# A decoder block with a PEER channel mixer on one Trainium2 core: groups of eight experts by column quarters, activations weighed and split in PSUM

## What is computed

```
q = a @ w_q                                   # a = rms_norm(h), 1024 tokens
s1, s2 = q0 @ k1.T, q1 @ k2.T                 # 8 heads, 128 keys each
top 16 of 128 x 128 sums per head -> idx, gate (softmax over the 16)
act = gelu(einsum('td,ted->te', xb, u[idx]))  # 128 experts of 16384 per token
out = einsum('te,ted->td', gate * act, v[idx])
```

## Time and profile before

| | us |
|---|---|
| median of 3 runs | 3580.4 |
| lowest, highest | 3580.07, 3585.87 |
| span of the profiled execution | 3575.0 |
| time of the median run less that span | 5.4 |
| mean granted TensorE clock, share of full | 0.983 |

### The profile page before, as it was taken

The page is one execution under the profiler, slowest core; times in us unless marked ns, Lnnn a source line. Parts: engine busy times, 40 slices in busy tenths (PEclk is TensorE's granted clock), DMA queues, the critical chain, the costliest instruction groups (busy, mean ns, idle before and its releaser), DMA issues.

```text
span 3575.0 us, 58964 instructions
## 1 busy us (share of the span) xinstructions
PE 3398.0 (95%) x22379; PEld 3333.7 (93%) x22379; DVE 2760.2 (77%) x4360; ACT 1201.3 (34%) x1885; POOL 2199.5 (62%) x1426
## 2 busy tenths in 40 slices
PE   7899989989999989999999999999999999999997
PEld 6899979988999979999999999999999999999975
DVE  5515467667887666999989899753898989998877
ACT  3310131232221232465665656542222222222242
POOL 5578865323678655666666666665666666666544
PEclk9999989999999999999999999999999999999998
DMA  4233432111688768889888988997888899988812
GB/s 152 79 117 123 136 108 79 56 49 65 215 311 313 279 217 290 281 307 326 310 324 303 335 304 323 322 354 258 314 309 312 310 312 314 315 311 311 282 60 94
DMA packets 326530, 856.15 MB, mean 239 GB/s; under 512 B 27856, under 2 KB 125648, under 8 KB 323024
## 3 DMA queue, kind: packets, MB, share of 16 engines
q0 software_dynamic: 110592, 402.70, 31.3%
q1 hardware_dynamic: 74592, 260.24, 21.5%
q10 hardware_dynamic: 141168, 190.87, 15.4%
HBM read 758.82 MB, written 94.90 MB: 239 GB/s over the span
## 4 chain that ended last, share of the span: by engine, by line
PE 71%; DVE 14%; issue 4%; DMA 3%; POOL 3%; ACT 3%; ACTq 1%; SPq 0%; DVEq 0%; POOLq 0%
PE main L720 52%; PE main L965 12%; PE scr L918 4%; DMA raw<-stream 3%; DVE scr L1729 2%; POOL v_lo L675 2%; POOL rows L626 1%; DVE rows L1722 1%; ACTq L1350 1%; DVE h L2104 1%; PE scr L818 1%; PE scr L735 1%; ACT v_hi L1360 1%; DVE res L2210 1%; DVE h_lo L2109 1%
## 5 line engine op out<-in xcount | busy, mean ns | idle before, releaser
L592 POOL TENSOR_TENSOR w_lo<-raw,w_hi 128x1024 fp32r<-128x1024 f32 x206 | 529.0, 2568 | 403.6 <-ACT w_hi L1064 397.7
L720 PE MATMUL main<-mix_hi,w_hi 128*128 128x320 f32 (+1 forms) x2816 | 684.7, 317 | 29.6 <-DVE mix_lo L1552 9.9
L720 PE MATMUL main<-mix_lo,w_hi 128*128 128x320 f32 (+1 forms) x2816 | 672.7, 313 | 0.0
L720 PE MATMUL main<-mix_hi,w_lo 128*128 128x320 f32 (+1 forms) x2816 | 672.6, 313 | 0.0
L626 POOL DMA_INDIRECT rows<-v_rows,s_idx x384 | 388.9, 1013 | 365.1 <-DVE scr L1729 290.9
L1729 DVE SCALAR_TENSOR_TENSOR scr<-rows,s_dot,scr 128x1024 f32<-128x1024 f32 x381 | 487.5, 1279 | 49.5 <-DMA rows<-v_rows,s_idx 31.5
L965 PE MATMUL main<-h_hi,v_hi 128*128 128x320 f32 x2048 | 473.2, 312 | 39.3 <-DVE res L2115 36.3
L720 PEld LDWEIGHTS main<-mix_hi,w_hi 128*128 128x128 f32 x2816 | 476.3, 189 | 34.0 <-issue 19.6
L720 PE MATMUL main<-a_hi,w_hi 128*128 128x320 f32 (+1 forms) x1728 | 466.7, 324 | 24.8 <-DVE a_lo L1552 8.8
L626 POOL DMA_INDIRECT rows<-u_rows,s_idx x384 | 399.0, 1039 | 137.0 <-issue 69.4
L720 PEld LDWEIGHTS main<-mix_lo,w_hi 128*128 128x128 f32 x2816 | 480.0, 189 | 0.0
(11 more groups left out here) (273 smaller groups left out, 5283.4 us busy)
## 6 DMA issues: line engine op xcount, KB each, us to landing
raw<-stream SPq DMA_DIRECT2D x478, 512.0 KB
act_d<-actb ACTq DMA_DIRECT2D x128, 320.0 KB
gate_d<-gbuf ACTq DMA_DIRECT2D x20, 2048.0 KB, 9.4
h<-act_d ACTq DMA_DIRECT2D x128, 320.0 KB
gate_in<-gate_d ACTq DMA_DIRECT2D x31, 1280.0 KB
rows<-u_rows,s_idx POOLq DMA_INDIRECT x384
rows<-v_rows,s_idx POOLq DMA_INDIRECT x384
score_d<-stage ACTq DMA_DIRECT2D x16, 320.0 KB
```

What stands on the lines that cost most here:

```text
L592: pool.tensor_tensor(w_lo[:, s, :], raw[:, s, :], w_hi[:, s, :].bitcast(F32), ALU.subtract) \
L720: last = pe.matmul(main[s][:, dst:dst + n], wt[:, s, c * P:(c + 1) * P], rows[:, c, src:src + n], start=(c == 0 and wt is w_hi and rows is ...
```

## The change

EG is 8: 16 groups, each of 8 column blocks ("steps", 128 in all) of 48 matmuls. V's tiles are laid out anew on the host: tile n of a group holds four experts by a quarter (256 columns) of the output, so a step pair needs two tiles, and only four tiles are held in v_hi and v_lo. h_hi, h_lo and h32 hold eight experts. Each expert's activations are copied by ACT into a PSUM place (`h_stage`, scr1), weighed there by DVE, cast from there by ACT, and the low half is the difference between it and h_hi. Gates are loaded for four experts at a time. All three sparse sums use scr0 and out0, and are turned into a place of `main` that counts as an item of its own between steps. Sparse rows before the V stage are 512, in it 256, with rings of 4 and 6 buffers. The first group's weighing moves into ACT's and DVE's loops at U tiles 119 to 126.

```diff
-EG = 4
+EG = 8
+HG = EG // 2
 NGRP = NE // EG
+V_STEPS = NGRP * DC
+PRE = 2
...
-LAST_ROWS = 2 * S1 + NE - 8
-SHIFT_ROWS = 2 * S1 + NE - 24
+LAST_ROWS = 2 * S1 + NE - 3
+SHIFT_ROWS = 2 * S1 + NE - 16
+FIRST_H = NE - EG - 1
+WEIGH_AT = ((), (0,), (1,), (2, 3), (4,), (5,), (6, 7), ())
+ROW_STEPS = V_STEPS - 5
 
 
...
-    return sum(RATES[:min(tile, LAST_ROWS)]) // 10
+    return min(sum(RATES[:min(tile, LAST_ROWS)]) // 10, UDOTS + P)
...
+def b_rows(step):
+
+    return A_DOTS + max(0, min(B_DOTS, B_DOTS * (step + 1) // ROW_STEPS))
...
+def target(step):
+
+    return UDOTS + P * (ENDS.index(step) + 1) if step in ENDS else b_rows(step)
...
+TURNS = [DC * ((ENDS[t] + 2 + DC) // DC) for t in range(NS - 1)] + [V_STEPS - 3]
...
-RING_B = (3, 4, 5, 7, 8, 9, 10, 11, 12)
+RING_END = (4, 5, 6, 7)
+RING_B = (4, 5, 8, 9, 10, 11)
...
-            v_hi.append(lay(f"v_hi{u}", [P, EG, D], F32R))
-            v_lo.append(lay(f"v_lo{u}", [P, EG, D], F32R))
+            at = set1 if u == 0 else set2
...
-            h32.append(nc.alloc_sbuf_tensor_at(f"h32_{u}", [P, EG, TDN], F32,
-                                               offset=(set1 if u == 0 else set2) + 42 * 1024))
-        gate_first = nc.alloc_sbuf_tensor_at("gate_first", [P, NBLK, EG, TB], F32, offset=tmp0)
-        v_raw = nc.alloc_sbuf_tensor_at("v_raw", [P, EG, D], F32, offset=set1 + 4 * K4)
...
             def fetch(n):
 
...
-                    while at_row[0] < to:
-                        gather()
+                to = min(target(n - 2) + 2, DOTS)
...
             pool.wait_ge(tile_done, 2 * B_PAIR)
-            pool.wait_ge(h32_ready, EG)
             for n in range(NE):
-                if n >= EG:
+                if n == PRE:
+                    pool.wait_ge(dot_done, A_DOTS)
+                if n >= PRE:
                     pool.wait_ge(v_hi_made, n + 1)
-                    pool.tensor_tensor(v_lo[n // EG % 2][:, n % EG, :], raw[:, n % 2, :],
-                                       v_hi[n // EG % 2][:, n % EG, :].bitcast(F32), ALU.subtract).then_inc(v_split, 1)
+                    pool.tensor_tensor(v_tile(v_lo, n), raw[:, n % 2, :], v_tile(v_hi, n).bitcast(F32),
+                                       ALU.subtract).then_inc(v_split, 1)
...
+            def turn_back(t):
...
+            def group(b, u, turns, last_turn=None):
                 for dt in range(DC):
-                    ahead_of(dt)
-                    slot = main[dt % 2]
-                    pe.wait_ge(b_drained, DC * b + dt + 1)
+                    if dt == last_turn:
+                        turn_back(turns)
+                        turns += 1
+                    quarter, of_two = divmod(dt, 2)
+                    slot = main[(dt + turns) % 2]
+                    pe.wait_ge(b_drained, DC * b + dt + turns + 1)
                     for k in range(EG):
+                        part, at = divmod(k, HG)
+                        n = 2 * quarter + part
+                        if of_two == 0 and at == 0:
+                            pe.wait_ge(v_split, EG * b + n + 1)
                         if dt == 0:
-                            pe.wait_ge(v_split, EG * b + k + 1)
                             pe.wait_ge(h_ready, EG * b + k + 1)
+                        col = at * 2 * P + of_two * P
                         for vt, ht in ((v_hi, h_hi), (v_hi, h_lo), (v_lo, h_hi)):
                             for half in range(2):
                                 last = pe.matmul(slot[:, half * HALF:half * HALF + HD],
-                                                 vt[u][:, k, dt * P:(dt + 1) * P],
+                                                 v_tile(vt, n)[:, col:col + P],
                                                  ht[u][:, k, half * HD:(half + 1) * HD],
                                                  start=(k == 0 and vt is v_hi and ht is h_hi),
                                                  stop=(k == EG - 1 and vt is v_lo))
                     last.then_inc(b_filled, 1)
...
             def v_cast(n):
-                b, k = divmod(n, EG)
-                act.wait_ge(raw_in[n % 2], 16 * (B_PAIR + (n - EG) // 2) + 16)
-                act.copy(v_hi[b % 2][:, k, :], raw[:, n % 2, :]).then_inc(v_hi_made, 1)
+                if n >= 4:
+                    act.wait_ge(b_filled, filled(2 * (n // 2 - 1)))
+                act.wait_ge(raw_in[n % 2], 16 * (B_PAIR + (n - PRE) // 2) + 16)
+                act.copy(v_tile(v_hi, n), raw[:, n % 2, :]).then_inc(v_hi_made, 1)
+
+            def h_stage(b, k):
+                act.wait_ge(act_in[k], 16 * b + 16)
+                if b or k:
+                    act.wait_ge(h_ready, EG * b + k)
+                act.copy(h_ps[:, 0:TDN], h32[b % 2][:, k, :]).then_inc(h_staged, 1)
 
             def h_cast(b, k):
                 act.wait_ge(h32_ready, EG * b + k + 1)
-                act.copy(h_hi[b % 2][:, k, :], h32[b % 2][:, k, :]).then_inc(hhi_ready, 1)
+                act.copy(h_hi[b % 2][:, k, :], h_ps[:, 0:TDN]).then_inc(hhi_ready, 1)
+                if k % HG == HG - 1 and b + 1 < NGRP:
+                    load_gates(b + 1, k // HG)
...
                 gelu(e)
+                if 0 <= e - FIRST_H < EG:
+                    h_stage(0, e - FIRST_H)
                 if e + 2 < NE:
                     after(A_PAIR + e // 2, e % 2)
+                if 0 <= e - FIRST_H < EG:
+                    h_cast(0, e - FIRST_H)
...
-            load_gates(1, gate_in)
-            act.wait_ge(dot_done, A_DOTS)
-            for k in range(EG):
-                load_act(1, k)
             act.wait_ge(gates_drained, 32 * ND + 2)
...
+            def sums_out(t):
+                act.wait_ge(dot_done, UDOTS + P * (t + 1))
...
+                act.copy(out0[:, :], acc[:, :]).then_inc(s_out, 1)
...
+            for b in range(NGRP):
+                for dt in range(DC):
+                    step = DC * b + dt
+                    if dt == 0 and b + 1 < NGRP:
+                        if b:
+                            act.wait_ge(b_filled, filled(step))
+                        for k in range(EG):
+                            load_act(b + 1, k)
+                    if step - 1 in ENDS:
+                        sums_out(ENDS.index(step - 1))
+                    ks = WEIGH_AT[dt] if b + 1 < NGRP else ()
+                    for k in ks[:1]:
+                        h_stage(b + 1, k)
+                    if dt % 2 == 0:
+                        for n in range(step + 2, min(step + 4, NE)):
+                            v_cast(n)
+                    for k in ks[:1]:
+                        h_cast(b + 1, k)
+                    for k in ks[1:]:
+                        h_stage(b + 1, k)
+                        h_cast(b + 1, k)
...
-                        acc = scr[ACC[t]]
+                        acc = scr[0]
...
             def weigh(b, k):
-                u = b % 2
-                gates = gate_in if b else gate_first
-                if k == 0:
-                    dve.wait_ge(gate_ins, 16 * (b + GATE_PARTS))
...
-                dve.tensor_tensor(h3, h3, gates[:, :, k, :], ALU.mult).then_inc(h32_ready, 1)
+                half = k // HG
+                if k % HG == 0:
+                    dve.wait_ge(gate_ins[half], 16 * (b + GATE_PARTS))
+                dve.wait_ge(h_staged, EG * b + k + 1)
+                h3 = h_ps[:, 0:TDN].rearrange("p (b t) -> p b t", t=TB)
+                dve.tensor_tensor(h3, h3, gate_in[half][:, :, k % HG, :], ALU.mult).then_inc(h32_ready, 1)
 
             def lo_of_group(b, k):
                 u = b % 2
                 dve.wait_ge(hhi_ready, EG * b + k + 1)
-                dve.tensor_tensor(h_lo[u][:, k, :], h32[u][:, k, :], h_hi[u][:, k, :].bitcast(F32), ALU.subtract) \
+                dve.tensor_tensor(h_lo[u][:, k, :], h_ps[:, 0:TDN], h_hi[u][:, k, :].bitcast(F32), ALU.subtract) \
...
-            def drain(b, dt):
...
+            def drain(step):
+                r = res[:, step % DC, TS:T].rearrange("p (a t) -> p a t", a=2)
+                dve.wait_ge(b_filled, 8 + item(step) + 1)
+                dve.tensor_tensor(r, main[item(step) % 2][:, :].rearrange("p (a t) -> p a t", a=2)[:, :, 0:HD], r,
+                                  ALU.add).then_inc(b_drained, 1)
 
...
             for k in range(EG):
+                rows_of(FIRST_H + k - 1)
                 weigh(0, k)
-            for k in range(EG):
+                dot_until(min(at_dot[0] + 1, A_DOTS))
                 lo_of_group(0, k)
...
+            dot(A_DOTS - at_dot[0])
+            weigh_sparse(2)
+
+            for step in range(V_STEPS - DC):
+                b, dt = divmod(step, DC)
+                if step in TURNS:
+                    add_sparse(TURNS.index(step))
+                drain(step)
+                for k in WEIGH_AT[dt]:
+                    weigh(b + 1, k)
+                    dot_until(min(at_dot[0] + 1, target(step)))
+                    lo_of_group(b + 1, k)
+                dot_until(target(step))
...
```

(29 more changed lines are left out.)

216 lines of the change are left out of this document (80 added, 136 removed).

## The result

The changed kernel takes 3611.9 us (median of 4 runs, 3604.47 to 3614.21); beside it, on the same chip, the kernel before takes 3580.35 us. The ratio is 1.0085, with a 95% interval of 1.0068 to 1.0102. The change makes the kernel slower by 0.9%, where 0.7% faster was forecast; the time lies outside the range.

The account below looks back on a forecast made before the run. TensorE, busy 95% of the 3575.0 us span, was taken as the bound, stopped by DVE's late drains. V stage -31.5, end of U +6, behind -1 gave 3548.5, plus 5.4 made 3554 us; range 3530 to 3583.

Parts of the forecast that it names:

- DVE relieved: V stage: halved drains and PSUM operands leave DVE 40.8 us of work in 56.3, so TensorE stops waiting for it.
- V supply: V stage: V tiles with thin margins in one or two places stop TensorE 1 us per group, 15 us (2 to 45).
- 3 us at the start of the stage: Start of V stage: eight act loads issued at once delay ACT's first V casts, 3 us (0 to 10).
- C: Rival, V stage: the supply of V through ACT, POOL and two raw slots sets the pace, 3595 us; chance 0.14.
- Turns: V stage: three turns of sparse sums, 2.6 us, plus 1 us each waiting for drain and row, 3 us (0 to 8).
- End of U: Last eight U tiles: later w_hi casts and more sparse rows cost about 1 us in six tiles, +6 us (0 to 20).
- rival D: End of U stage: linked ACT, DVE and POOL waits start four of eight tiles 7 us late, +28, 3576 us; chance 0.10.
- Behind the stage: After the V stage: two additions of squares left instead of three, one waiting for its square, -1 us (0 to -2).
- 5.4 us from span to median: Whole kernel: the median of the runs, 3580.4 us, stands 5.4 us over the profiled span; added to the forecast span.

Follow-up runs that it names:

- e1: Changed kernel with ACT making its two V casts ahead of the eight act loads at each group's first step: 3590.6 us, ratio 1.0020 to before.
- e4: Changed kernel with weighing, cast and low half back in SBUF, without the PSUM place or ACT's staging copy: 3593.1 us, ratio 1.0036 to before.
- e7: Changed kernel with weighing, cast and low half in SBUF and ACT's V casts ahead of the act loads: 3566.5 us, ratio 0.9952 to before.

## Why the prediction was wrong, step by step

**DVE relieved: right.** Weighing and low half cost 0.828 and 0.820 us against 0.815 priced; drains are halved; TensorE's waits for res are 7.4 us, under the 10 named. DVE is busy 64 of 100 us, less than the 70 to 75 foreseen.

**V supply, 15 us (2 to 45): the step that failed.** TensorE waited 30.4 us for v_lo by the rows, and by the starts of the steps the stage lost 59.1 - 10.5 = 48.6 us beside the turns, which passes the upper bound of 45. About 12 us of it are half clock behind the stops. The text had put some 13 us of before down to the clock and to the stops' edges, and its sum for after has no such term. Two mechanisms made the stops. The first was in its text and priced once only: the eight act loads were given 3 us at the start of the stage, from a row of 4.48 us for four, and the steady state, where the same eight stand ahead of the casts in each of 15 groups, got nothing. The start of the stage, which got the 3 us, had no stop; in the groups behind it the runs show 10.8 us of standing on average, and 35 us lost by TensorE, which e1 takes away. The second is the chain at the PSUM place. It was followed with a row of 1.3 us in it, as if each row had landed; DVE's waits for rows were 9.8 us before and are 197.7 now. The text put the worst margin at step 6, and a stop was there: 8.8 us, or 0.55 a group. The larger ones were at steps 1 and 2, and, with these mended, 3 and 4.

**C's mechanism.** C priced the cycle of raw slots, and 15.0 us for a pair of tiles (960.7/64) is what it had. But ACT waited for raw tiles 39.7 us instead of 380.2: the slots were not short, ACT came late. C had ACT's queue in its text but priced the slots: that it hit the size was luck.

**Turns, 5.6 us (2.6 + 3): 10.5 measured**, so the second term is 7.9, at its bound of 8. The step behind the second turn, 8.93 us, loses 1.9 more at half clock. The longest wait for a drain comes where the drain stands behind a row that has not landed.

**End of U, +6 (0 to 20): +26.4, the other step that failed.** This is rival D, priced at +28 and given 0.10, and its mechanism of linked waits was there. Missing from it was ACT standing 12 us in the gate loads. They had gone out one a tile and now went out four a turn, and the sum had no term for that. D's reason against, a tile of slack in each wait, was wrong, since POOL's gathers stand ahead of the next w_lo. D did not come instead of the forecast but with C's loss in V, which the cases, taken as exclusive, gave no chance.

**Behind the stage, -1: +4.6.** The chain there, from the last matmuls on:

```profile
3433.11 7.31 PE main L1015 x48
...
3440.45 0.82 DVE res L2173
3441.28 1.32 DVE p_lo L2204
3442.60 2.84 DVE rowb L1580
...
3447.50 3.26 DVE rowb L1583
...
3456.78 0.75 DVE res L2173
...
3457.57 4.63 PE main L1057 x12
```

The squares that moved ahead of the last two drains (L1580, L1583) take 2.84 and 3.26 us instead of 1.24, while POOL splits the weights that it now starts earlier, and the last drain ends 3 us after the last matmul of the V stage, which ends at 3454.50. That POOL stretches them is a reading only; no run took it away. e4 (153.3) has less of it and shows no reason.

**5.4 us from span to median: not what it looked like.** Where a run lists both, its time is 1.9 us over its span (3612.6 and 3610.7 for the changed kernel). So 3.5 of the 5.4 us are the difference between the profiled execution of before and its usual ones; it had no stop in U tiles 70 to 93, and whether the others had is open, as they left no trace.

## What to carry to other kernels

When a tile size doubles, the bursts of DMA issues double too, and an issue is not free for the engine that makes it: put the issues behind the work that others wait for. Before paying for a cheaper operation with a chain through one buffer, see whether the larger tile has already given that engine its slack. A stage's second cause is hidden behind the first one: mend them together before either is judged: e1 and e4 alone stayed slower than before, and e7 did not.
